# A feed-forward in half blocks: order of loads and stores, late rows one by one, additions spread, weight sums on VectorE

## The reference

```python
        x = x + jnp.sum(gates * branches, axis=2) @ w_out[l]

        h2 = rms_norm(x, norm_ffn[l])
        x = x + (jax.nn.silu(h2 @ w_ffn_gate[l]) * (h2 @ w_ffn_up[l])) @ w_ffn_down[l]
```

## Time and profile before

| | us |
|---|---|
| runs: median (lowest to highest) | 3265.19 (3258.33 to 3266.27) |
| profiled execution | 3261.54 |
| its span in the profile | 3259.7 |
| TensorE busy | 3104.6 |
| ScalarE busy | 1332.9 |
| POOL busy | 811.5 |

### The profile page before, as it was taken

One profiled execution on the slowest core, in us unless ns is written; L12 is line 12 of the kernel. 1 busy time (PEld: TensorE's weight loads), 2 busy tenths in 40 slices (PEclk: granted clock), 3 DMA queues, 4 the chain that ended last, 5 costly groups with the idle time before them and its releaser, 6 DMA issues. The chain is left out here.

```text
span 3259.7 us, 50403 instructions
## 1 busy us (share of the span) xinstructions
PE 3104.6 (95%) x18600; PEld 2629.8 (81%) x18600; DVE 1740.3 (53%) x3480; ACT 1332.9 (41%) x2640; POOL 811.5 (25%) x994
## 2 busy tenths in 40 slices
PE   7999999999999999998898888998999999999999
PEld 7988889999998888886677677776987777687777
DVE  6567683433454133256555455796343566753776
ACT  5456564444453222133222222444343555622452
POOL 3424334344440000011333332160011110023131
PEclk9999999999999999999999999999999999999999
DMA  5010001111113121131222223743210000122012
GB/s 198 34 46 21 33 21 59 43 48 58 50 50 101 49 75 49 55 136 41 83 86 79 94 81 113 246 140 132 70 45 18 23 15 26 68 82 88 27 54 102
DMA packets 77412, 231.27 MB, mean 71 GB/s; under 512 B 17712, under 2 KB 21936, under 8 KB 65648
## 3 DMA queue, kind: packets, MB, share of 16 engines
q1 hardware_dynamic: 77168, 228.05, 19.8%
HBM read 183.92 MB, written 43.84 MB: 70 GB/s over the span
## 5 line engine op out<-in xcount | busy, mean ns | idle before, releaser
L2470 PE MATMUL ps<-whi,hhi 128*128 128x256 f32 (+2 forms) x1920 | 580.0, 302 | 2.2 <-ACT ig L2718 0.8
L2470 PE MATMUL ps<-whi,hlo 128*128 128x256 f32 (+2 forms) x1920 | 563.8, 294 | 0.0
L2470 PE MATMUL ps<-wlo,hhi 128*128 128x256 f32 (+2 forms) x1920 | 563.4, 293 | 0.0
L2470 PEld LDWEIGHTS ps<-whi,hhi 128*128 128x128 f32 x1920 | 368.1, 192 | 12.2 <-ACT ig L2718 1.8
L2470 PEld LDWEIGHTS ps<-wlo,hhi 128*128 128x128 f32 x1920 | 368.5, 192 | 7.3
L2470 PEld LDWEIGHTS ps<-whi,hlo 128*128 128x128 f32 x1920 | 367.9, 192 | 7.6
L2470 PE MATMUL ps<-hhi,whi 128*128 128x512 f32 x864 | 342.6, 397 | 0.0
L2470 PE MATMUL ps<-hhi,wlo 128*128 128x512 f32 x864 | 337.3, 390 | 0.0
L2470 PE MATMUL ps<-hlo,whi 128*128 128x512 f32 x864 | 336.6, 390 | 0.0
L3069 POOL CAST whi<-raw 128x512 fp32r<-128x512 f32 (+4 forms) x172 | 108.8, 632 | 651.1 <-PE ps L2470 641.7
L3080 POOL TENSOR_SCALAR stats<-stats 128x2 f32<-128x2 f32 (+2 forms) x230 | 60.1, 261 | 829.9 <-DVE stats L2841 353.4
(11 more groups left out here) (549 smaller groups left out, 7234.6 us busy)
## 6 DMA issues: line engine op xcount, KB each, us to landing
raw<-in_W SPq DMA_DIRECT2D x61, 1024.0 KB, 4.8
wf<-in_WF SPq DMA_DIRECT2D x22, 1024.0 KB, 4.8
scratch_fs<-fo SPq DMA_DIRECT2D x77, 256.0 KB, 2.0
raw<-in_W SPq DMA_DIRECT2D x24, 768.0 KB, 4.2
wd<-in_WD SPq DMA_DIRECT2D x44, 256.0 KB, 3.4
scratch_x<-x SPq DMA_DIRECT2D x16, 512.0 KB, 3.1
orw<-scratch_outs SPq DMA_DIRECT2D x6, 1024.0 KB, 5.6
xin<-in_x SPq DMA_DIRECT2D x8, 512.0 KB, 10.6
```

What stands on the lines that cost most here:

```text
L2470: x = e.matmul(r.out, a, b, start=(r.start and m == 0), stop=(r.stop and m == n - 1), skip_group_check=r.joined)
```

## The change

1. Weight sums of the strips and of the down product are made by VectorE (`combine(False, ...)` for `True`). The sums of outputs at the end of a pair stay on POOL.
2. In the strips, the load of strip i + 2 is issued behind `p4` of strip i, and the stores of a pair stand behind `end` in `keep_sums`; those of the last pair come at step 3 of the down product.
3. Rows 4 to 7 are made one after the other, both halves of a row together (`by_row`). Their `t3` turns are made later, by `turn_t3`, among the first products. `WeightSet` has two placings, one for the first two strips. Set 0 is loaded before the tiles as before; set 1 only behind the last of them. The order of the first two strips is written anew.
4. `prepare` of the down product's first two steps comes later in the last strip. `down_add` takes at most two targets at a time. `w_split` moves to steps 52 and 63, and the loads behind it to steps 56 and 67.
5. `m2_split` is made in two halves at steps 73 and 74; of the last `down_add` only one target remains behind the last step, as before; the bank rotation is moved on by four.

The diff, cut to its core:

```diff
@@ row_tiles
             for t0 in (0, 4):
+                if t0 and by_row:
+                    for t in range(4, 8):
+                        for j in range(2):
+                            p = DB.take()
+                            m = some(t, p, chunks[j](), numbered(t), len(blocks(t)))
+                            add(t, j, p)
+                            if j:
+                                pend.append(finish(t))
+                            tick()
+                        by_row(t)
+                    for ch in chunks[0]() + chunks[1]():
+                        ch.done(m)
+                    continue
@@ WeightSet.sums
-                sum1 = combine(True, s1, a21, a22, ALU.add, self.landed, free[0])
+                sum1 = combine(False, s1, a21, a22, ALU.add, self.landed, self.done[4], *free)
...
@@ norm_row
-            three = combine(False, xs[:, early], xs[:, late], xs[:, early], ALU.subtract)
+            t3_of[t] = x1[:, t, early] if t < 6 else xs[:, early]
+            three = combine(False, t3_of[t], late, xs[:, early], ALU.subtract, x1_kept[t] if t < 6 else None)
             yield
-            p = row_T(xs[:, late], t, r.scaled, [w[:, 4:8, :] for w in hpair])
             q = row_T(h_diff[u % 2][:, :], t, one)
-            s = row_T(xs[:, early], u, three, (t3h, t3l))
+            if t == 7:
+                turn_t3(7)
+            else:
+                p = row_T(late, t, r.scaled, [w[:, 4:8, :] for w in hpair])
...
+        def first_weights(t):
+            if t == 4:
+                sets[0].sums(0)
+                sets[0].split(0, 0, 1, free=scr.free)
+            elif t < 7:
+                sets[0].split(0, *((4, 2) if t == 5 else (5,)), free=scr.free)
+        sets[0].load(0, raw_free)
         x_last = row_tiles(chunks, ..., norm_row, True, by_row=first_weights)
+        sets[1].load(1, x_last)
+        sets[1].sums(1, x_last)
@@ Strips.end
-                fo_free[1] = [fs_store(1, k, fo_made[1]), sum4]
...
+                self.stored = [(1, fo_made[1]), (3, fo_made[3]), (4, sum1), (2, sum3), (5, sum2), (6, sum4)]
+            def keep_sums(self):
+                k = self.i // 2
+                for j, ready in self.stored:
+                    fo_free[j] = fo_free[j] + [fs_store(j, k, ready)]
@@ the first two strips, the new order
         s0.p1()
         s0.keep()
+        turn_t3(4)
+        turn_t3(5)
+        s0.p2()
+        tick()
+        turn_t3(6)
+        turn_t2(0)
+        tick()
+        s0.p5()
+        tick()
...
+        turn_t2(1)
+        sets[0].split(0, 3, 6, free=x_last)
+        s0.p7()
+        turn_t2(2)
+        turn_t2(3)
+        sets[1].split(1, 0, 1, free=x_last)
+        s1.p1()
+        s1.keep()
+        t4_full = [turn_t4(u) for u in range(2)]
+        s0.gate_early()
+        s0.p6()
+        t4_full += [turn_t4(u) for u in range(2, 4)]
...
+        s0.u3()
+        s0.c22()
+        s1.p2()
+        sets[1].split(1, 4, 2, free=x_last)
         s0.p4()
         sets[0].load(2)
+        s0.c21()
         s0.p3()
+        s0.end()
         sets[0].sums(2)
+        sets[1].split(1, 5, 3, 6, free=x_last)
         s1.gate_early()
         s1.p6()
+        s1.p7()
         s1.p5()
         s1.u3()
...
         s1.p4()
+        sets[1].load(3)
@@ the steady loop
             if more:
-                other.load(i + 1)
                 other.sums(i + 1)
             s.p1()
...
             s.p4()
+            if i + 2 <= last_strip:
+                here.load(i + 2)
             s.c22()
             if more:
                 other.split(i + 1, 1, 2)
             else:
-                prepare(1)
+                prepare(0)
...
             s.end()
+            if i % 2 and more:
+                s.keep_sums()
@@ prepare (the same for t3, t2, t4)
-                made = combine(True, b.raw, at_("12"), at_("11"), ALU.subtract, got("12", "11"), b_free)
+                made = combine(False, b.raw, at_("12"), at_("11"), ALU.subtract, got("12", "11"), b_free)
@@ the steps of the down product
+            if i == 3:
+                s.keep_sums()
...
+                    pair = [targets[x:x + 2] for x in range(0, len(targets), 2)]
+                    adds = [(p - 1, before, n, x) for n in range(4) for x in pair]
...
-            if before and k < 4:
-                down_add(p - 1, before, k)
+            if adds:
+                down_add(*adds.pop(0))
...
-            if s in (50, 56):
+            if i in (52, 63):
                 w_split()
+            if i in (56, 67):
+                w_load()
+            if i == 69:
                 t_m2 = load("mem2", m2r[:, :, :], d["mem2T"], t_split[3])
+            if i in (73, 74):
+                m2_free = t_split[7]
+                m2_lo = m2_split(i - 73)
...
+        DB_ALL.i = (DB_ALL.i + 4) % 6
         for n in range(4):
-            down_add(6, before, n)
+            down_add(6, before, n, (1,))
```

More of the change, by code:

```diff
@@ new lines, in __init__, with operands @@
+                self.done = [None] * 7
+            def operands(self, name, raw_at, sums_at, hi_at):
+                o = Rec()
+                o.raw4 = at(name, [4, 512], F, raw_at)
+                lo4 = at(f"{name}l", [4, 512], R, raw_at)
+                sums = at(f"{name}s", [3, 512], F, sums_at)
+                lo3 = at(f"{name}sl", [3, 512], R, sums_at)
+                o.raw = [o.raw4[:, j, :] for j in range(4)] + [sums[:, j, :] for j in range(3)]
+                o.lo = [lo4[:, j, :] for j in range(4)] + [lo3[:, j, :] for j in range(3)]
+                o.hi = [at(f"{name}h{j}", [512], R, a)[:, :] for j, a in enumerate(hi_at)]
+                return o
@@ new lines, in of, with load, sums @@
+            def of(self, i):
+                return self.first if i < 2 else self.then
+            def load(self, i, *free):
+                self.landed = load(f"wf{self.x}", self.of(i).raw4[:, :, :], d["WF"][i], *free, self.done[:4])
+            def sums(self, i, *free):
+                a11, a12, a21, a22, s1, s2, s4 = self.of(i).raw
+                sum1 = combine(False, s1, a21, a22, ALU.add, self.landed, self.done[4], *free)
+                sum3 = combine(False, a21, a11, a21, ALU.subtract)
+                sum2 = combine(False, s2, s1, a11, ALU.subtract, self.done[5])
+                sum4 = combine(False, s4, a12, s2, ALU.subtract, self.done[6])
@@ new lines, in norm_row, with turn_t3 @@
+            two = combine(False, x0[:, early], x0[:, early], t3_of[t], ALU.add, row_full[u])
+            four = combine(False, x0[:, sl(512, 512)], x0[:, sl(512, 512)], x0[:, early], ALU.subtract)
+            late_ops[u] = (two, four)
+            if t == 7:
+                yield
+                p = row_T(late, t, r.scaled, [w[:, 4:8, :] for w in hpair])
+                h_read["b22"].append(p.read)
+            xsf_free[t % 2] = flat(p.full, two, three)
+        def turn_t3(t):
+            p = row_T(t3_of[t], t - 4, t3_made[t], (t3h, t3l), free=x_last)
+            h_read["t3"].append(p.read)
+            t3_full[t] = p.full
@@ L1700, in build @@
         s1.end()
+        s1.keep_sums()
         last_strip = 2 * FF_PAIRS - 1
@@ L1850, in build @@
                 rhs = [(lambda _, w=w: w) for w in (b.hi, b.lo)]
-                m = mm3(place, place.ps[:, :], lhs, rhs, 1, b_made[s], a_made[s], last=end, start=k == 0, stop=end, step=done)
+                m = mm3(place, place.ps[:, :], lhs, rhs, 1, b_made[i], a_made[i], last=end, start=k == 0, stop=end, step=done)
             a.free = b.free = done or m
-            if before and k < 4:
-                down_add(p - 1, before, k)
+            if adds:
+                down_add(*adds.pop(0))
                 if p == 6:
```

191 lines of the change are left out of this document (77 added, 114 removed).

## The result

| | before | after |
|---|---|---|
| median of four runs (lowest to highest), us | 3263.57 (3258.33 to 3266.27) | 3154.39 (3153.57 to 3155.22) |
| profiled execution, us | 3261.54 | 3155.22 |
| its span in the profile, us | 3259.7 | 3153.4 |

The ratio is 0.9667, with a 95% interval from 0.9651 to 0.9684: 109 us or 3.3% faster. The forecast was 3156, the range 3138 to 3191.

A forecast was written before the change was run, and what follows sets the result against it. TensorE, busy 95% of the span, was taken as the bound, so only its idle or lower-clock time could pay. Savings 0 + 84 + 14 + 8 = 106 from 3261.5 gave 3155.5, forecast 3156 us; range 3138 to 3191.

The forecast's parts named there:

- Strips 2 to 21: Strips 2 to 21: loads issued earlier, ahead of stores, save 84 of 87.5 us of loss, with 3 kept.
- the cover: Even strips, VectorE: `u3` ready at S+13.1 (S: strip start), product 4 wants it at S+13.6; 0.5 us to spare.
- Rivals 1 and 2: Even strips: 1, VectorE the bound, `u3` 2 us late, 3189, chance 0.14; 2, full exclusion, 0.7 late, 3162, chance 0.08.
- Rival 4: Strips: sums at the head of VectorE's order wait for late-landing weights; slower, 3272 at 6.1 us lost per strip; chance 0.03.
- Front: Last rows, strips 0 and 1: 69 us against 67.8, less 1 for an earlier end; nothing gained, bounds 7 gained, 6 lost.
- The three holes: TensorE idle: some 7 us before product 5, 2.6 before strip 1's first product, 6.7 before its product 6; 17 in all.
- Down product: 77 steps of the down product: saves 14 of 24 us of loss in four places; bounds 7 and 20.
- (a): Down product's start, 5 steps, 7 us lost: stores moved to step 3; a hole of 3.4 and slow spell remain; saves 2.
- (b): Down product, steps 15 and 16, 3.1 us lost: additions spread two by two over eight steps; saves 3.
- (c): Down product, steps 34 to 39, 7 us lost: weight sums moved from POOL to VectorE; saves 7.
- (d): Down product, steps 53 to 61, 6.6 us lost: load four steps later, nothing held; 4 us of overrun remain; saves 2.6.
- Hand-over: Hand-over to the second block: earlier halves of `m2` and an empty bank for the first product; saves 8 us (4 to 11).

The follow-up runs named there:

- e2: Changed kernel with the loads of strips 4 to 21 back behind the pair's stores, weight sums still on VectorE; median 3241.92 us, ratio 0.9932.
- e3: Changed kernel with late strip loads (behind the stores) and the strips' weight sums back on POOL, both at once; median 3228.75 us, ratio 0.9894.
- e4: Changed kernel with three more VectorE operations in every even strip from 2 on, behind the split of operand 6; median 3175.25 us, ratio 0.9727.
- e8: Changed kernel with the 44 weight sums of the down product back on POOL; median 3152.46 us, ratio 0.9661.
- e6: Changed kernel with set 1's last splits before product 3 of strip 0, ahead of the sums of strip 2; median 3148.33 us, ratio 0.9646.
- e1: Changed kernel with the four weight sums of every strip back on POOL, loads still early; median 3162.28 us, ratio 0.9689.
- e9: Changed kernel with all additions of one output tile in one step again, up to four a step; median 3157.74 us, ratio 0.9678.
- e10: Changed kernel with the second 1 MB load of later weights issued in step 73 instead of step 67; median 3151.54 us, ratio 0.9657.
- e12: Changed kernel with only the weight sums of the down product's fifth and sixth products back on POOL; median 3150.43 us, ratio 0.9656.
- e13: Changed kernel with later set 1 sums, earlier set 1 splits, 1 MB load at step 73, fifth and sixth products' sums held back on POOL; median 3141.8 us, ratio 0.9627.

## Why the prediction was right

**Strips 2 to 21 (84 predicted, 86.3 measured).** The chain through VectorE came out to within 0.1 us: first sum ended S+4.1, fourth S+9.2, operand 6 S+10.9, `u3` S+13.07. `e2` and `e3` show that the early load carries it, `e4` that the cover is 0.5 us, as predicted. What I kept back as 3 us of loss was 1.2. One step was off without harm: the landing, by the median 5.2 us after the issue instead of the 4.8 of the earlier trace rows.

**Rivals 1 and 2** fall with the same rows. The colliding operations take 1.66 to 1.67 each, as in the earlier trace rows, and start 1.70 apart in the even strip shown above. The Trainium skill's rule of full exclusion (page "SBUF — State Buffer", section "Who interferes with whom") would have put `u3` 0.7 us behind its time in these strips; the trace has `u3` at S+13.07 and no wait there at all. Half of a sign of being wrong did come: VectorE is busy 17.53 us of the even strip, where I had named 17 or more, but the waits for `fU` that were to come with it did not. What that section says of one-input instructions the trace agrees with: two additions with one operand in PSUM took 1.42 us in `e8`, in the middle of a row of six sums on POOL, as they do alone.

**Rival 4**, late landing, did not come. In one strip of nineteen the first sum was released by a landing, which I had named as a sign of being wrong. It cost nothing, since odd strips have no sums of outputs and VectorE is busy 13.94 of 19 us in that one. `e2` shows the mechanism at work when the loads are late.

**Front (0 predicted, 0.7 measured).** The three holes were foreseen with 17 us in all and measured with 15.8. The chain of row 7 was 1.3 us longer than I had it (product 5 started 17.6 us behind the end of the tiles, not 16.3), mostly the landing of set 1 at 7.0 instead of 6.2, while the holes in it were shorter. `e6` shows that the longest hole was nothing but an order on VectorE: `end` of strip 0 and the sums of strip 2, made there 19 us before that strip begins, stood ahead of a split that TensorE waited for. The row tiles were to end about 1 us earlier. They end 1493.3 us into the span in both kernels, and since that point moves by up to 4 us between the kernels, a gain of 1 can't be seen. No run sets the new order of the rows and first strips against the old one.

**Down product (14 predicted, 12.3 measured).** The total hides misses of either sign, of up to 3 us. (a) Steps 0 to 4 take 15.7 us, 2.1 over their floor: 4.9 saved, not 2. The hole of 3.4 and the slow spell behind it did not come; step 1 lost 1.4 and step 2 0.7 at full clock. Part of this is luck: step 1 took 4.1 us here and up to 5.3 in the experiments that leave it alone. In `e1` and `e2` its wait was 2.4 and 2.3 us, the clock fell to 0.50 behind it and step 2 took 4.1; in `e4` and `e6` a wait of 2.3 brought no spell. (b) Steps 15 and 16 lost nothing, as predicted; `e9` shows that spreading did it. (c) Steps 34 to 39 lost 0.6 and so saved 6.4, where I had 7. But the same load on VectorE comes again at steps 48 to 50, where additions of two targets meet a weight sum, and lost 1.6, which my sum did not have. (d) The hold on SyncE is gone from step 59, and steps 57 to 66 lost 4.8, where I had 4. A step with two low parts, a sum and two additions took 3.76 us, not 3.6: I had multiplied 0.69 and left out the 0.03 to 0.1 between instructions. (e) Steps 71 and 72 lost 2.3 behind the moved 1 MB load. I had written that the load comes "four steps later, with nothing held"; it held no issue, but what was issued behind it landed late, and `e10` shows it; in `e8` the same load at the same step cost nothing, so it takes more than the load. That is the one step of the prediction that failed in kind.

**Weight sums of the down product.** The prediction credited the move to VectorE with 7 us in (c). `e8` shows that the move as a whole is worth nothing (3152.46 against 3154.39, a difference that "all else" alone can make): it saved some 6 us at steps 34 to 39 and lost as much at 48 to 66. The sum by places was right, since (d) had the cost; the credit to the edit was not.

**Hand-over (8 predicted, 7.7 measured).** The empty bank and the early halves of `m2` gave the first product at once. As predicted, the turns of `x` behind it wait for each low part as before (2.32, 1.28, 1.25 us). No run takes the two halves of `m2` and the empty bank apart.

## What to carry to other kernels

In these strips the place of a load was worth 70 to 85 us and the engine of the sums 8 either way. On an engine that executes in order, write a load ahead of the stores of unrelated data, and an operation that waits for a transfer behind those that don't, or a late transfer stops all of them. An engine with spare time isn't free of cost if it has no wait to hold it: in `e8` and `e12` POOL's work ran ahead into steps that were already full, and VectorE's low parts took 1.66 us beside it instead of 0.69. Before an operation goes to another engine, add up each step's work against the step's length in every phase, with large loads' followers in the sum as well: in `e8`, `e12` and `e13` a loss removed in one phase was in good part made again in another.

## What the hardware showed beside that

- A 256 KB load issued right behind a 1 MB load landed 8.8 us after its issue, 4.2 without it. In the ten other experiments with this 1 MB load it took 7.1 to 9.0 us, in `e13`, without it, 4.5. In `e10` two such loads issued behind the 1 MB load of `mem2T` took 7.9 and 7.1.
- The median landing of a 1 MB weight load rose from 4.8 to 5.2 us in the changed kernel, where it is issued ahead of the stores; in `e2`, behind them again, it is 4.9 to 5.0. One load in the strips took 6.9.
- Nine holes of 1.54 us, one in every second strip, left TensorE's granted clock at 1.00, while a front with holes of 1.8, 0.9, 2.6 and 6.8 us came to 0.87.
- Two low parts of 128x1024 on VectorE took 3.10 us together beside sums on POOL. The sum that ran over the end of the second and into the next low part took 2.37 us instead of 1.30.
